# Half 1 of the second feed-forward product: octet 1 in seven products instead of eight

## The reference, cut to what matters

```python
h = _rmsnorm(x, ln2_w[l])
u = jax.nn.relu(jnp.einsum("bsd,df->bsf", h, w_ff1[l]))     # 2048 -> 8192
x = x + jnp.einsum("bsf,fd->bsd", jnp.square(u), w_ff2[l])  # 8192 -> 2048
```

## Time and profile before

| | us |
|---|---|
| median of three runs | 1503.49 |
| the profiled execution | 1503.49 |
| its span | 1501.8 |
| PE busy | 1494.7 |
| DVE busy | 1144.0 |
| ACT busy | 811.1 |
| DMA queue of SyncE, share of 16 engines | 62.4% |
| PE's granted clock | 1.00 |

### The profile page before, as it was taken

How to read it: one execution, slowest core, us unless ns; L and a number is a source line. 1 busy time by engine, 2 the same in 40 slices (tenths; PEclk the granted TensorE clock), 3 DMA queues, 4 the chain that set the end, 5 groups by cost and what they waited for, 6 DMA issues and landing times.

```text
span 1501.8 us, 19558 instructions
## 1 busy us (share of the span) xinstructions
PE 1494.7 (100%) x7470; PEld 1258.7 (84%) x7470; DVE 1144.0 (76%) x1363; ACT 811.1 (54%) x917; POOL 126.0 (8%) x161
## 2 busy tenths in 40 slices
PE   9999999999999999999999999999999999999999
PEld 7888888888888888888888888888888888888787
DVE  6877756878777877776666777778989566578978
ACT  6555444676664544544444545456656445465654
POOL 5000000000041100100000112110000111110000
PEclk9999999999999999999999999999999999999999
DMA  8678897744555444445799888766877656666884
GB/s 293 216 256 295 302 346 272 241 146 167 169 168 164 145 140 146 145 155 197 261 321 325 270 287 298 248 228 217 297 270 261 193 191 196 188 217 224 303 292 147
DMA packets 156825, 345.37 MB, mean 230 GB/s; under 512 B 8272, under 2 KB 8784, under 8 KB 153424
## 3 DMA queue, kind: packets, MB, share of 16 engines
q1 hardware_dynamic: 148960, 317.09, 62.4%
q0 software_dynamic: 6528, 25.17, 4.7%
q10 hardware_dynamic: 1264, 2.13, 0.4%
HBM read 317.11 MB, written 27.26 MB: 229 GB/s over the span
## 4 chain that ended last, share of the span: by engine, by line
PE 92%; DVE 3%; DMA 3%; ACT 0%; issue 0%; SPq 0%; DVEq 0%; ACTq 0%
PE banks L610 45%; PE banks L986 16%; PE banks L1032 10%; PE banks L989 8%; PE banks L1054 7%; DVE lo L2173 2%; DMA raw<-in_w_ff 2%; PE banks L626 1%; DVE t_sums L2204 1%; DMA early_sum<-in_w_ff 1%; PE banks L883 1%; PE banks L892 1%; DMA raw<-w_sums 1%; PE banks L767 1%; PE banks L740 1%; PE banks L647 0%
## 5 line engine op out<-in xcount | busy, mean ns | idle before, releaser
L1548 DVE TENSOR_TENSOR lo<-raw,hi 128x1024 fp32r<-128x1024 f32 x383 | 471.9, 1237 | 251.7 <-ACT hi L1087 250.0
L1087 ACT ACTIVATE hi<-raw 128x1024 fp32r<-128x1024 f32 x383 | 404.7, 1059 | 436.5 <-PE banks L610 257.1
L610 PE MATMUL banks<-hi,st 128*128 128x512 f32 x1584 | 498.9, 396 | 0.5 <-DVE lo L1548 0.5
L610 PEld LDWEIGHTS banks<-hi,st 128*128 128x128 f32 x1584 | 289.5, 188 | 55.7 <-DVE lo L1548 1.1
L986 PE MATMUL banks<-st,hi 128*128 128x512 f32 x1024 | 321.6, 395 | 0.0
L610 PE MATMUL banks<-lo,st 128*128 128x512 f32 x792 | 309.0, 390 | 0.0
L989 PEld LDWEIGHTS banks<-st,lo 128*128 128x128 f32 x1024 | 192.4, 188 | 45.4
L1498 ACT ACTIVATE hi<-raw 128x1024 fp32r<-128x1024 f32 x160 | 168.9, 1060 | 109.3 <-PE banks L1054 62.2
L2173 DVE TENSOR_TENSOR lo<-raw,hi 128x1024 fp32r<-128x1024 f32 x160 | 192.7, 1222 | 20.4 <-ACT hi L1498 14.6
L989 PE MATMUL banks<-st,lo 128*128 128x256 f32 x1024 | 201.2, 278 | 0.0
L610 PEld LDWEIGHTS banks<-lo,st 128*128 128x128 f32 x792 | 148.7, 188 | 31.8
(11 more groups left out here) (308 smaller groups left out, 1648.3 us busy)
## 6 DMA issues: line engine op xcount, KB each, us to landing
raw<-in_w_ff SPq DMA_DIRECT2D x116, 1024.0 KB, 5.5
raw<-in_w_in SPq DMA_DIRECT2D x99, 1024.0 KB, 5.0
raw<-w_sums SPq DMA_DIRECT2D x24, 1024.0 KB, 5.0
raw<-in_w_out SPq DMA_DIRECT2D x16, 1024.0 KB, 7.4
early_sum<-in_w_ff SPq DMA_DIRECT2D x12, 1024.0 KB, 8.0
w_sums<-early_sum SPq DMA_DIRECT2D x12, 1024.0 KB, 10.0
late_sum<-in_w_ff POOLq DMA_DIRECT2D x12, 1024.0 KB, 6.5
w_sums<-late_sum POOLq DMA_DIRECT2D x12, 1024.0 KB, 5.5
```

Of the source, the lines that this page charges most:

```text
L610: last = pe.matmul(acc[:, t], w[:, k0 + 2 * m + kk, P * t:P * t + P], v[:, (i + more) % PIECES, kk, :], start=m == 0 and kk == 0 and a == ...
L1087: act.activation(hi[:, (i + more) % PIECES], raw[:, i // 2 % RAW, 2 * (i % 2):2 * (i % 2) + 2, :], ACT.Copy)\
L1548: dve.tensor_tensor(lo[:, (i + more) % PIECES], raw[:, i // 2 % RAW, 2 * (i % 2):2 * (i % 2) + 2, :], hi[:, (i + more) % PIECES].bitcast(F ...
```

## The change

Half 1 stores octet 1 too: its sevens are 0, 1, 2, 3, 5, 6 and only 4 and 7 stay plain. There are 28 half octets of stored sums instead of 24; the additional four are made in the first product of half 0, where steps now come every four pieces (261 to 301) instead of every seven or eight (261 to 308). POOL's loop takes as many of them per group as fall in it. u of octet 1 needs 14 KB instead of 8, so the homes of half 1 move; octet 7's goes to 80 KB, in `st`. The plain octets' fourth bank begins at octet 4 instead of 1.

```diff
-STORED = ((0, 3, 6), (0, 3, 6))
+STORED = ((0, 3, 6), (0, 1, 3, 6))
-STORED_OCTETS = [(half, np_, o) for half in (1, 0) for np_ in range(2) for o in STORED[half]]
-SUM_STEPS = [20, 28, 36, 44, 51, 56, 61, 66, 71, 76, 81, 86, 227, 234, 240, 245, 251, 261, 268, 276, 284, 292, 300, 308]
+STORED_OCTETS = [[(half, np_, o) for np_ in range(2) for o in STORED[half]] for half in range(2)]
+STORED_OCTETS = STORED_OCTETS[1][:6] + STORED_OCTETS[0] + STORED_OCTETS[1][6:]
+SUM_STEPS = [20, 28, 36, 44, 51, 56, 61, 66, 71, 76, 81, 86, 227, 234, 240, 245, 251,
+             261, 265, 269, 273, 277, 281, 285, 289, 293, 297, 301]
...
-            at = (100, 128, 114, 168, 136, 182, 196, 214)
+            at = (100, 114, 128, 168, 214, 182, 196, 80) if half else (100, 128, 114, 168, 136, 182, 196, 214)
...
-                    if half == 0:
+                    if 2 * n >= EARLY_STEPS:
...
-                if h < len(SUM_STEPS):
+                while h < len(SUM_STEPS) and SUM_STEPS[h] < 8 * (QF0 + o + 1):
...
-                            begins = o == 1 and j == 1 and t == 1
+                            begins = o == first_plain and j == 1 and t == 1
```

More of the change, by code:

```diff
@@ L1040, in plain @@
                 a0 = piece0(half) + octet0(half, np_, o)
+                first_plain = next(o for o in range(OCTETS) if o not in SEVENS[half])
                 if np_ == 0:
```

## The result

The changed kernel takes 1519.86 us (median of five, 1518.35 to 1520.66) against 1503.39 us (five runs, 1502.10 to 1504.35): ratio 1.0106, 95% interval 1.0094 to 1.0117. It is slower by 16.5 us; 8.7 were forecast. The sign is right, the size is outside the range.

A forecast was written before the change was run, and what follows sets the result against it. PE was busy 1494.7 of 1501.8 us, but DVE had no room in octets 0 to 3 of half 1's second product. -2.7 + 5.3 + 6.1 = +8.7 us on 1503.49 gave 1512 us, range 1503 to 1518.

The forecast's parts named there:

- (a): PE's matmuls: two octets have 42 instead of 48, -2.7 us, all that the change can gain.
- (b): Half 1's first product: one more `token_sums` on POOL and its split on ACT and DVE, hidden, 0 us.
- (c): Half 0's first product: four more stored half octets on DVE, POOL and DMA; taken as 0, upper bound 5 us.
- R3: Rival: half 0's first product is starved as well, the forecast and the 5 us of (c), 1517 us; chance 0.12.
- (d): Half 1's second product: octet 2's four local sums on DVE stand between splits at octets 1 and 2, +5.3 us.
- (e): Half 1's second product: octet 1's `w_sums` tiles and octet 2's tiles come late, +6.1 us beyond (d), bounds 0 and 13.
- R1: Rival, half 1's second product: tiles come in time and only (d) bites, +2.6 us, 1506.1 us; chance 0.17.
- R2: Rival, half 1's second product: DVE has 3.65 us of slack at the sums, nothing stalls, -2.7, 1500.8 us; chance 0.08.
- R4: Rival: seven pieces save no matmul time, since a piece of six matmuls waits for lo; 1515 us, chance 0.05.
- three terms: DVE's added busy time: 6 more splits (7.3 us), 12 instructions of stored sums (10.4), a split of u's sums (1.2).

## Why the prediction was wrong, step by step

- **(a) -2.7 us of matmuls.** Right. With the burst and the tiles out of the way octets 0 to 3 take 38.1 and 38.3 us, against 39.7 and 39.8 before.
- **(b) Half 1's first product, 0.** Right: 178.3 us in both.
- **(c) The stored sums, 0 with an upper bound of 5.** This step failed, and it is the main reason for the miss. It cost 4.8 us in the profile and 6.0 us by the run of the sums alone. The demand, 376 GB/s, was worked out right, and about 350 came; what I did with them was wrong. I wrote that the lead of the tiles and of POOL's chain covers the shortage. The weights' tiles do have 16.7 us, and no row waits for them. But a stored sum has far less: write, landing, read and its landing must fit in 22.3 us beside DVE's three instructions and POOL's turns, and POOL starts no other transfer while it waits for a write, so a write must land well within 11.1 us. With writes that take 10.8 us in the median and reads that take 8.5 it does not fit. "It fits if the write keeps its 5.5 us" was the condition, the traffic in the same paragraph put it in doubt, and I did not put the two together. The upper bound came from throughput alone. It gave 5 us, the profile 4.8, but that is luck in part: the same stage took 184.1 to 186.8 us in five profiles, 4.8 to 7.6 more than before. Whether POOL's chain would have broken with less traffic in all, no run tells. Rival R3, which named this place and this chain, had 0.12 of the chance and a price of 5 us; it is what happened, at 1517 by its sum, 1519.86 measured.
- **(d) The burst, +5.3 us.** 7.2 us by the run without it (4.1 + 3.1). The pace of 2.27 us for 1.36 and the last three waits, 1.0 us each, are nearly as derived (0.91). That the lead at the sums was near nothing and not 1.5 us, since the late tiles had used it up, fits this but was not measured by itself.
- **(e) The tiles, +6.1 us.** The 6.0 us that (d) leaves of 13.2. The size is right, the detail is not: the wait of 1.3 us that I put at piece 10 of the first pass came at piece 11, since the first stored tile was in time and the second 1.3 us late.
- **(d) and (e) together, +11.4 us.** Measured 6.9 + 6.3 = 13.2 us over what the matmuls need. Before, the same octets had lost 0.2 and 0.3 us, so 12.6 us are new; with the matmuls' 2.7 off that is 9.9. Behind octet 3 the passes got 0.9 us shorter and 0.3 longer, which I had not foreseen, and so the profile has 9.2 us net (from the times before rounding). That it comes so near my 8.7 is partly luck; by the medians of the run without the additional sums half 1 costs 10.2.
- **The miss in all.** Measured 16.5 us, forecast 8.7: 6.0 of the 7.8 us between are (c), 1.5 half 1, and 0.3 is left open.
- **R1** (the tiles in time) is refuted by the waits for `w_sums` and for octet 2's tiles. The Trainium skill ("DMA: Bandwidth & Descriptors", section Anatomy of one DMA) gives the fit behind my estimate of 4.4 us, 2.0 us and the bytes at 436 GB/s, for transfers that GpSimd issues. The trace does not bear it out for these tiles, which go through SyncE's queue: in the first pass octet 1's stored tiles landed 5.0 and 7.2 us after their issue, octet 2's 7.6 and 9.1.
- **R2** (the gain arrives) needed 3.65 us of slack; the waits at pieces 14 to 17 in both passes show that it was not there. **R4** is refuted: 168 matmuls in seven took 38.1 us where nothing held them up.
- The growth of DVE's busy time, 19 us forecast, was 22.6. The three terms measured 11.0, 6.4 and 1.2 us, as forecast; the rest lies in longer records of the splits of u, for which I have no cause.

## What to carry to other kernels

An engine that is 90% busy over a stretch can still be the bound in it: compare it with the pace of the consumer in each short stretch, and count the lead in buffers, here four pieces and 1.5 us. Work that is free behind a slow step (a plain octet) is paid in full behind a fast one, so making a step faster removes cover from what stands beside it; moving the octet cost 12 us with no work added. And a chain of transfers in one queue, each waiting for the landing of the last, can fail while other transfers beside it are still in time: set its period by the landings of the loaded stage, not of the quiet one.

## What the runs showed of the hardware that I had not expected

- A full DMA share alone does not tell how late a transfer lands. In the change's trace (853 to 950 us) six 1 MB writes were issued 0.7 to 2.2 us behind a read of the same queue and landed after 10.7 to 12.2 us; two were issued 3.9 us behind one and landed after 5.9 us (a ninth, 5.8 us behind, after 7.1). While those two were under way 393 and 384 GB/s moved at a share of 1.02 and 0.99, more than the 350 of the longer stretches. The run of the sums alone has the same two groups (11.0 to 12.2 us, and 5.7 and 6.3). In the kernel before, at a share of 0.83, a write landed after 5.1 us. Whether it is the read just ahead that makes a write late no run isolates; with sums every five pieces writes issued 4.0 to 4.3 us behind a read took 6.9 to 9.9 us.
- A quarter of the bytes did not mean a quarter of the time: in the median of that stage 256 KB writes landed after 6.3 us, 1 MB writes after 10.8.
- A stage at the edge is also unsteady. With sums every four pieces the same stage took 184.1, 184.4, 184.5, 185.5 and 186.8 us in five profiles; without the shortage it took 179.2 us in every profile. The nine runs of the sums alone spread over 8.8 us, or 4.0 without the slowest.
